# A hybrid SSD, attention and PEER layer: the query/key/value projection, its norm, rotation and transposes as one stage, with modulation units on four column groups

## The reference

```python
mod_ctx = jax.nn.silu(c_ctx) @ w_ada[l] + b_ada[l]          # 6 parts of 1024: shift1, scale1, gate1, shift2, scale2, gate2
mod_lat = (jax.nn.silu(c) @ w_ada[l] + b_ada[l])[:, None, :]
h = modulate(rmsnorm(x, lp['norm1_w']), shift1, scale1)
proj = h @ lp['w_in']                                        # z, xbc, dt_f, dt_b, q, k, v, g_a, g_b
q = rmsnorm(q.reshape(bsz, t, N_HEADS, HEAD_DIM), lp['q_norm_w'])
k = rmsnorm(k.reshape(bsz, t, N_KV_HEADS, HEAD_DIM), lp['k_norm_w'])
if ctx_k is None:                                            # context rows: no rotation, k and v are outputs
    keys, vals = k, v
else:
    q = axial_rope(q, pos[0], pos[1])
    keys = jnp.concatenate([axial_rope(k, pos[0], pos[1]), ctx_k], axis=1)
    vals = jnp.concatenate([v, ctx_v], axis=1)
y_b2 = attend(q, keys, vals) @ lp['w_attn_out']
```

## Time and profile before

| | us |
|---|---|
| median of 3 runs | 3220.26 (3216.32 to 3221.43) |
| the profiled execution | 3218.21 |
| its span, first to last instruction | 3216.4 |
| PE busy | 2690.7 (84%) |
| PEld busy | 2341.4 (73%) |
| DVE busy | 2256.1 (70%) |
| ACT busy | 1026.3 (32%) |
| POOL busy | 715.5 (22%) |
| stage 1 | 0 to about 57.4 |
| stage 2 | 57.4 to 184.6 |
| stage 3 | 184.6 to 302.9 |

### The profile page before, as it was taken

One profiled execution on the slowest core, in us unless ns is written; L12 is line 12 of the kernel. 1 busy time (PEld: TensorE's weight loads), 2 busy tenths in 40 slices (PEclk: granted clock), 3 DMA queues, 4 the chain that ended last, 5 costly groups with the idle time before them and its releaser, 6 DMA issues. The chain is left out here.

```text
span 3216.4 us, 41637 instructions
## 1 busy us (share of the span) xinstructions
PE 2690.7 (84%) x15241; PEld 2341.4 (73%) x15241; DVE 2256.1 (70%) x3693; ACT 1026.3 (32%) x1411; POOL 715.5 (22%) x597
## 2 busy tenths in 40 slices
PE   4968999998899999487767506679999999999995
PEld 3956777776777777377757506669998899988995
DVE  2252666665167777533329997769999999999997
ACT  3111444443233332322122105723333333333332
POOL 0000000000166666100000005623223333233330
PEclk7976999999999999788878758989999999999998
DMA  4253111111332332444210102399999999999995
GB/s 194 86 196 116 43 57 73 56 49 66 129 121 91 109 100 79 163 151 153 93 72 27 40 0 105 170 386 409 405 402 401 397 399 399 400 403 396 402 399 210
DMA packets 157182, 638.82 MB, mean 199 GB/s; under 512 B 13639, under 2 KB 77511, under 8 KB 93579
## 3 DMA queue, kind: packets, MB, share of 16 engines
q1 hardware_dynamic: 117676, 360.60, 30.2%
q0 software_dynamic: 39104, 276.71, 21.1%
q10 hardware_dynamic: 288, 0.03, 0.0%
HBM read 569.21 MB, written 68.21 MB: 198 GB/s over the span
## 5 line engine op out<-in xcount | busy, mean ns | idle before, releaser
L2022 POOL DMA_INDIRECT p_uv<-in_uv_rows,sidx x256 | 331.3, 1294 | 738.7 <-DVE p_ys L2174 661.7
L2036 PE MATMUL p_pa<-h2D,w_hi 128*128 128x384 f32 x1024 | 345.5, 337 | 15.5 <-PEq L2258 14.9
L2038 PE MATMUL p_pa<-h2D,w_lo 128*128 128x384 f32 x1024 | 344.9, 337 | 0.0
L2037 PE MATMUL p_pa<-h2D,w_hi 128*128 128x384 f32 x1024 | 344.7, 337 | 0.0
L104 DVE TENSOR_TENSOR w_lo<-w_raw,w_hi 128x2048 fp32r<-128x2048 f32 x64 | 152.3, 2383 | 267.2 <-ACT w_hi L99 267.0
L2174 DVE SCALAR_TENSOR_TENSOR p_ys<-p_uv,p_sw,p_ys 128x1024 f32<-128x1024 f32 x256 | 328.9, 1285 | 9.2
L2073 ACT ACTIVATE w_hi<-w_raw 128x2048 fp32r<-128x2048 f32 x126 | 241.5, 1917 | 273.8 <-PE p_py L2052 244.4
L2160 DVE CUSTOM_DVE_ANT_0 p_uv<-p_uv,hrow 128x1024 f32<-128x1024 f32 x256 | 307.3, 1219 | 14.4 <-DMA p_uv<-in_uv_rows,sidx 14.4
L2050 PE MATMUL p_py<-w_hi,p_wh 128*128 128x512 f32 x768 | 304.4, 396 | 7.3 <-DVE w_lo L2138 7.3
L2138 DVE TENSOR_TENSOR w_lo<-w_raw,w_hi 128x2048 fp32r<-128x2048 f32 x126 | 288.4, 2289 | 29.6 <-ACT w_hi L2073 29.6
L2051 PE MATMUL p_py<-w_lo,p_wh 128*128 128x512 f32 x768 | 305.1, 397 | 0.0
(11 more groups left out here) (341 smaller groups left out, 6075.5 us busy)
## 6 DMA issues: line engine op xcount, KB each, us to landing
w_raw<-in_w_stream SPq DMA_DIRECT2D x190, 1024.0 KB, 7.5
g_dram<-e_st SPq DMA_DIRECT2D x6, 4096.0 KB, 11.3
p_g<-g_dram SPq DMA_DIRECT2D x64, 384.0 KB, 16.2
q_ada<-in_w_ada SPq DMA_DIRECT2D x16, 1024.0 KB, 4.9
xc_dram<-c_xc SPq DMA_DIRECT2D x8, 1284.0 KB, 4.5
m_ada<-in_w_ada SPq DMA_DIRECT2D x6, 1024.0 KB, 19.5
s_xx<-xc_dram SPq DMA_DIRECT2D x8, 642.0 KB, 5.6
s_bc<-xc_dram SPq DMA_DIRECT2D x8, 642.0 KB, 7.0
```

The lines of the kernel that those rows point to most:

```text
L2022: nc.gpsimd.indirect_dma_start(uv[:, k % RING, :], None, K.uv_rows, bass.IndirectOffsetOnAxis(K.sidx[:, t, c:c + 1], 0)).then_inc(K.gather ...
L2036: nc.tensor.matmul(ps_a[m][:, :], wh[:, k, cols], K.h2D[0][:, k, :], start=k == 0, stop=False)
L2037: nc.tensor.matmul(ps_a[m][:, :], wh[:, k, cols], K.h2D[1][:, k, :], start=False, stop=False)
L2038: mm = nc.tensor.matmul(ps_a[m][:, :], wl[:, k, cols], K.h2D[0][:, k, :], start=False, stop=k == KD - 1)
```

## The change

Stages 2 and 3 become one, and nothing goes through `qkv_dram`.

- The dt weights are loaded and split in stage 1, into the free high and low buffers of slot 1. The high part of unit 1 is therefore made after the dt matmuls.
- As soon as a tile of a pair is in PSUM, ACT squares it there (`square`), DVE reduces, ACT takes the root (`root`), and DVE scales from PSUM and rotates (`normed`). POOL has multiplied the rotation tables with the norm weights before, so the rotated tiles need no product with the weight; the context tile has one. A piece is 8 query heads (pairs 0 and 1), or 4 key heads (pair 2, whose other half are the values, copied by ACT).
- PE transposes a piece in four blocks (`transposes`), at places in its queue that the table `follows` fixes: pieces 0 to 4 of a pair after the pair's tile 4 and after tiles 0, 2, 3 and 4 of the unit behind it. What has no such place is in `tail`. Two PSUM buffers take turns, and ACT evacuates them (`evacuate`).
- The 16 modulation units come in four batches of four (`rows`), all in row form on four column groups: after units 0, 1, 3 and 5, in the order shift2, scale2, gate1, gate2. Batches 0 and 1 are copied to SBUF and transposed (piece `COLS`), and DVE makes columns of them; batches 2 and 3 are the gates. SP loads each batch as a whole after the one before is used, in one queue with the stream's loads. The gates leave in eight stores.
- In stage 1 three of the eight buffers for modulation units are parts of `QT` and `KT`, which are allocated earlier.

```diff
-    ada = [K.raw[0], K.raw[1]] + [sb(f"m_ada{i}", [P, 8 * UC]) for i in range(6)]
+    qt, kt = K.QT[:, :, :].rearrange("p k t -> p (k t)"), K.KT[:, :, :].rearrange("p k t -> p (k t)")
+    ada = ([K.raw[0], K.raw[1], qt[:, 0:8 * UC], qt[:, 8 * UC:16 * UC], kt[:, 0:8 * UC]]
+           + [sb(f"m_ada{i}", [P, 8 * UC]) for i in range(3)])
+    dtw = sb("m_dtw", [P, KD * 64])
...
+            sp.dma_start(dtw[:, :], K.w_dt).then_inc(dtw_in, 16)
...
+                if t == 2:
+                    act.wait_ge(dtw_in, 16)
+                    nc.scalar.activation(K.whi[1][:, 0:KD * 64], dtw[:, :], ACT.Copy).then_inc(dtw_hi, 1)
...
+                if t == 3:
+                    dve.wait_ge(dtw_hi, 1)
+                    nc.vector.tensor_tensor(K.wlo[1][:, 0:KD * 64], dtw[:, :], K.whi[1][:, 0:KD * 64].bitcast(F32),
+                                            ALU.subtract).then_inc(dtw_lo, 1)
...
 def phase_tokens(nc, K, ctx):
...
-    ob = [sb(f"t_ob{t}", [P, 2 * UC]) for t in range(NT)]
+    PARTS = (3, 4, 2, 5)
-    ps_dt = ctx.enter_context(nc.psum_tensor("t_psdt", [P, NT, 64], F32))
-    ps_cum = [ctx.enter_context(nc.psum_tensor(f"t_cum{i}", [P, 3, NT * HEADS], F32)) for i in range(2)]
+    ps_row = ctx.enter_context(nc.psum_tensor("t_row", [P, 2 * UC], F32))
+    ps_dt = ps_row[:, 0:NT * 64].rearrange("p (t c) -> p t c", t=NT)
+    ps_t = [ctx.enter_context(nc.psum_tensor(f"t_pt{i}", [P, 4, P], F32)) for i in range(2)]
+    ps_cum = [ps_t[i][:, :, :].rearrange("p a c -> p (a c)")[:, 0:3 * NT * HEADS].rearrange("p (r x) -> p r x", r=3) for i in range(2)]
+    ada = [sb(f"t_ada{j}", [P, KD * UC]) for j in range(4)]
...
+    chunk = lambda i, t: 1 + NT * i + t
+    COLS = 1 + NT * PAIRS
+    AT = (4, 5, 7, 8, 9)
+    follows = {(1, 0): [0], (2, 1): [COLS]}
+    tail = []
+    for i in range(PAIRS):
+        for t in range(NT):
+            n = NT * (2 * i + 1) + AT[t]
+            if n < NT * N_TOK:
+                follows.setdefault((n // NT, n % NT), []).append(chunk(i, t))
+            else:
+                tail.append(chunk(i, t))
+    ORDER = [g for u in range(N_TOK) for t in range(NT) for g in follows.get((u, t), [])] + tail
+    turn = {g: n for n, g in enumerate(ORDER)}
...
+            def ada_load(b):
+                if b:
+                    sp.wait_ge(ada_used, b)
+                for j in range(4):
+                    sp.dma_start(ada[j][:, :], K.w_ada[4 * PARTS[b] + j]).then_inc(ada_in[j], 16)
...
+            ada_load(0)
...
+            S.load(sp, 3, 1)
+            ada_load(1)
+            S.load(sp, 4, 0)
+            S.load(sp, 5, 1)
+            ada_load(2)
+            S.load(sp, 6, 0)
+            S.load(sp, 7, 1)
+            ada_load(3)
+            S.load(sp, 8, 0)
+            sp.wait_ge(grow_done, 1)
+            for j in range(4):
+                for i in range(2):
+                    sp.dma_start(K.gates[0:2, i * D + j * UC:i * D + (j + 1) * UC], b_row[32 * j:32 * j + 2, i * UC:(i + 1) * UC]).then_inc(g_out, 16)
...
-            act.wait_ge(dtw_in, 16)
-            nc.scalar.activation(dtwh[:, :, :], dtw[:, :].rearrange("p (k c) -> p k c", k=KD), ACT.Copy).then_inc(dtw_hi, 1)
-            S.hi(act, 1, 1)
+            def square(i, t):
+                act.wait_ge(mm_done, NT * i + t + 1)
+                n = (QH if i < 2 else KH) * HD
+                nc.scalar.activation(sq[t % 2][:, 0:n], ps[t][:, 0:n], ACT.Square).then_inc(sq_done, 1)
+                if i == 2:
+                    nc.scalar.activation(K.vals[:, t, :], ps[t][:, n:2 * UC], ACT.Copy).then_inc(v_done, 1)
+            def root(i, t):
+                c = NT * i + t
+                act.wait_ge(ms_done, c + 1)
+                n = QH if i < 2 else KH
+                nc.scalar.activation(ss[c % 2][:, 0:n], ss[c % 2][:, 0:n], ACT.Sqrt).then_inc(rt_done, 1)
+            def evacuate(g):
+                n = turn[g]
+                act.wait_ge(tr_done, n + 1)
+                nc.scalar.activation(out, ps_t[n % 2][:, :, :], ACT.Copy).then_inc(tr_ev, 1)
...
+            act.wait_ge(dt_mm, 1)
+            S.hi(act, 1, 1)
             act.wait_ge(cum_mm, 2)
+            S.hi(act, 2, 0)
+            for i in range(PAIRS):
+                square(i, 0)
+                square(i, 1)
+                if i == 0:
+                    evacuate(0)
+                root(i, 0)
+                square(i, 2)
+                root(i, 1)
+                square(i, 3)
+                root(i, 2)
+                evacuate(chunk(i, 0))
+                square(i, 4)
+                S.hi(act, 2 * i + 3, 1)
+                if i == 0:
+                    act.wait_ge(ada_used, 2)
+                    nc.scalar.activation(row[:, :], ps_row[:, :], ACT.Copy).then_inc(row_ev, 1)
+                root(i, 3)
+                evacuate(chunk(i, 1))
+                root(i, 4)
+                if i == 0:
+                    act.wait_ge(modc_done, 2)
+                    act.sem_inc(tr_ev, 1)
+                for t in range(2, NT):
+                    evacuate(chunk(i, t))
+                if i < PAIRS - 1:
+                    S.hi(act, 2 * i + 4, 0)
...
+            def normed(i, t):
+                c, g = NT * i + t, chunk(i, t)
...
+                dve.wait_ge(sq_done, c + 1)
+                link(nc.vector.tensor_reduce(s, heads(sq[t % 2][:, 0:n * HD]), axis=AX.X, op=ALU.add))
+                nc.vector.tensor_scalar(s, s, 1.0 / HD, EPS, ALU.mult, ALU.add).then_inc(ms_done, 1)
+                dve.wait_ge(rt_done, c + 1)
+                link(nc.vector.reciprocal(s, s))
+                nc.vector.tensor_tensor(heads(x), heads(ps[t][:, 0:n * HD]), s.unsqueeze(2).to_broadcast([P, n, HD]),
+                                        ALU.mult).then_inc(x_read, 1)
+                dve.wait_ge(x_read, c + 1)
+                if turn[g] >= 3 and g >= 4:
+                    dve.wait_ge(tr_done, turn[g - 3] + 1)
...
+                axes = x.rearrange("p (h a f d) -> p h a f d", h=n, a=2, f=2)
+                a, b = axes[:, :, :, 0, :], axes[:, :, :, 1, :]
+                for f, (j, op) in enumerate(((0, ALU.subtract), (1, ALU.add))):
+                    link(nc.vector.tensor_tensor(t1[:, 0:n], a, tab(0, j), ALU.mult))
+                    link(nc.vector.tensor_tensor(t2[:, 0:n], b, tab(1, 1 - j), ALU.mult))
+                    last = nc.vector.tensor_tensor(qo[:, :, :, f, :], t1[:, 0:n], t2[:, 0:n], op)
+                    if f == 0 or i == 2:
+                        link(last)
+                    else:
+                        last.then_inc(src_done, 1)
+                if i == 2:
+                    nc.vector.tensor_copy(kd[:, :, 1, :], kd[:, :, 0, :]).then_inc(src_done, 1)
...
+            nc.vector.memset(ps_row[:, :], 0.0).then_inc(row_zero, 1)
...
+            S.lo(dve, 1, 1)
+            dve.wait_ge(cum_exp, 2)
...
+            for i in range(PAIRS):
+                for t in range(4):
+                    normed(i, t)
                 S.lo(dve, 2 * i + 3, 1)
+                normed(i, 4)
+                if i == 0:
+                    dve.wait_ge(small, 32)
+                    dve.wait_ge(tr_done, turn[COLS] + 1)
+                    for b in range(2):
...
+                if i < PAIRS - 1:
+                    S.lo(dve, 2 * i + 4, 0)
+            dve.wait_ge(brow_in, 8 * 16)
+            dve.wait_ge(ada_used, 4)
+            nc.vector.tensor_tensor(b_row[:, :], ps_row[:, :], b_row[:, :], ALU.add).then_inc(grow_done, 1)
...
+            def rows(b):
+                for j in range(4):
+                    pe.wait_ge(ada_in[j], 16 * (b + 1))
+                for kd in range(KD):
+                    for j in range(4):
+                        nc.tensor.matmul(ps_row[32 * j:32 * j + 2, b % 2 * UC:(b % 2 + 1) * UC], K.silu_c[:, kd, :],
+                                         ada[j][:, kd * UC:(kd + 1) * UC], start=(kd == 0), stop=(kd == KD - 1))
+                pe.drain().then_inc(ada_used, 1)
+            def transposes(g):
+                n = turn[g]
+                if g == 0:
+                    pe.wait_ge(ck_done, 2)
+                elif g == COLS:
+                    pe.wait_ge(row_ev, 1)
+                else:
+                    pe.wait_ge(src_done, g)
+                if n >= 2:
+                    pe.wait_ge(tr_ev, n - 1)
+                for j in range(4):
+                    if g == 0:
+                        src = ckd[:, j, :, :].rearrange("p c d -> p (c d)")
+                    else:
+                        src = (row if g == COLS else qr[g % 3])[:, j * P:(j + 1) * P]
+                    mm = nc.tensor.transpose(ps_t[n % 2][:, j, :], src, K.ident[:, :])
+                mm.then_inc(tr_done, 1)
+            def unit(u):
+                i, s = u // 2, u % 2
+                S.ready(pe, u)
                 wh, wl = (x[s][:, :].rearrange("p (k c) -> p k c", k=KD) for x in (K.whi, K.wlo))
                 for t in range(NT):
-                    if s == 0 and not isinstance(i, int):
```

(34 more changed lines are left out.)

349 lines of the change are left out of this document (109 added, 240 removed).

## The result

| us | before | after |
|---|---|---|
| median (range, executions) | 3219.5 (3216.3 to 3221.4, 4) | 3126.2 (3125.2 to 3130.3, 4) |
| profiled execution (span) | 3218.2 (3216.4) | 3125.2 (3123.5) |
| projection's start to attention's first instruction | 245.5 | 151.5 |
| everything behind that | 2913.5 | 2914.3 |

The ratio is 0.971, 95% interval 0.970 to 0.973: faster. The forecast was 3128.0 with 3116 to 3145 around it. The time that was saved lies wholly in the stretch that the prediction marked off: 245.5 - 151.5 = 94.0 us. Of these 0.4 us came back ahead of it, where the stage before ended later, and 0.8 us behind it.

A forecast was written before the change was run, and what follows sets the result against it. PE was taken to bound the projection. One TensorE queue to 192.05 us, then a DVE tail, starts attention at 210.7 instead of 302.9: 3220.3 - 92.2 = 3128 us, range 3116 to 3145.

The forecast's parts named there:

- the 0.7 wait: Pair 0, before the fourth tile's transposes: PE waits about 0.7 us for the modulation columns, the stage's tightest place.
- The bound: Merged stage up to unit 5: one TensorE queue sets the time, ending at 192.05 us with unit 5's transposes.
- The rival that DVE is the bound: Merged stage: at 6.0 us a DVE tile, 10 to 14 us longer, 3140; chance 0.13.
- Transposes: PE's queue before the last batch: 13 groups of four transposes at 0.7 us each, 9.1 in all.
- the lower bound of 6.5: PE's queue: low end for all 13 transpose groups, at 0.5 us each; the upper end was 13.
- all waits hidden: PE's queue: the low case for one group of four transposes, 0.5 us.
- the 13.7 in the text: PE's queue: time charged for unit 1 from its start at 104.25, in placing PE's wait at 136.7.
- the rival: Modulation loads arrive late, at 4.9 us per 1 MB: 6 us more, 3134; chance 0.06.
- The slow rival: Row batches and transposes hold PE's clock down from 86 us to unit 5's end: 106 us more, 3234; chance 0.03.
- closed no circle: Rival on ACT's queue: waits for PE and DVE prevent overlap, 30 to 35 us come back, 3160; chance 0.06.
- Tail: Stage's end: DVE late, needing 3.9 us a tile against 2.86; gate rows added at 205.1, attention at 210.7.
- The handover: Stage's end: 3.5 us from the last gate store to attention, after 2.1 for seven more store issues.

The follow-up runs named there:

- Experiments 7: Kernel after with the rotation of the query heads left out, so less DVE work: 3125.5 us.
- experiment 4: Kernel after with the two loops of a row batch exchanged, so each column group finishes its unit before the next begins: 3154.4 us.
- Experiments 1 to 3: Kernel before with row-form batches in the old third stage, 3198.0 us; then ACT's row copy moved, 3197.0; then three batches' loads left out too, 3179.6.
- Experiment 5: Kernel after with the third to fifth transposes of pairs 0 and 1 earlier in PE's queue: 3141.5 us.
- experiment 3: Kernel before with row-form batches in the old third stage, ACT's copy moved, and only the first batch's weights loaded: 3179.6 us.
- experiment 2: Kernel before with row-form batches in the old third stage, all loads kept, ACT's row copy moved behind a root: 3197.0 us.
- experiments 5 and 7 to 10: Kernel after with: transposes earlier, 3141.5 us; query rotation out, 3125.5; key rotation out too, 3125.4; unit 7's split later, 3125.8; also first gates and root earlier, 3123.2.

## Why the prediction was right

The forecast's terms and the trace (us):

| step | forecast | trace after |
|---|---|---|
| PE's first matmul | 57.45 | 57.83 |
| dt matmuls | 25.6 | 25.6 |
| unit 0, sums, batch 0 | 15.7 + 1.6 + 3.9 | 15.6 + 1.8 + 3.9 |
| unit 1 starts | 104.25 | 104.72 |
| four transposes inside a unit / at its end | 0.7 / 0.7 | 0.35 / 0.5 to 0.7 |
| PE waits for the modulation columns | 0.7 | 0.50 |
| DVE tile, eight heads / four | 4.9 / 3.9 | 4.77 / 3.73 |
| lo of unit 6 starts | 180.4 | 178.15 |
| unit 5 begins | 177.9 | 175.43 |
| unit 5 and its transposes end | 192.05 (192.8 with the 0.7 wait, which the sum left out) | 190.11 |
| gate rows added | 205.1 | 202.73 |
| first store to attention | 5.6 | 6.5 |
| attention starts | 210.7 | 209.25 |

- **The bound.** Until unit 5 the stage is PE's queue, as forecast. Experiments 7 (DVE work out: nothing) and 4 (PE work in: all of it, and more) show it from both sides. The rival that DVE is the bound falls; it also rested on PSUM as a source, and that costs nothing here.
- **Transposes.** They were sized too high. Between two tiles the matmul at 107.51 and the next of the unit at 107.98 are 0.47 apart, 0.12 of it the pitch, so four transposes cost 0.35 us and not 0.7. The prediction charged 0.16 for the matmul ahead to finish; the rows show the transpose starting one pitch behind it (107.63), with no such end to wait for. Seven of the eight groups in such places cost 0.35 each, and the one that waits for ACT 0.55 beside its wait. The five at a unit's end, with its drain, cost 0.5 to 0.7 beyond the 0.25 that the end costs anyway. That is some 6.1 us for the 13, where 9.1 were charged, and less than the lower bound of 6.5: what was taken as "all waits hidden", 0.5 a group, was still too high. This is why unit 5 begins 2.5 us earlier than forecast, although unit 1 began 0.5 later and took 0.5 longer than the 13.7 in the text.
- **Loads.** A load of 1 MB of a batch landed 10.5 us after its issue in the median and 14.6 at most, and no matmul waited for `t_ada`. Asked for at 104.54, 132.19 and 165.91, as forecast (104.3, 132, 166.6), they are wanted at 119.8, 155.6 and 190.1. Experiments 1 to 3 show what the rival would have looked like: where nothing of the projection lies between asking for a batch and using it, the loads cost 16 us, the low clock behind PE's waits included.
- **Clock.** It was 1.0 from 98 us to the tail. The slow rival did not come: row batches and transposes between the units do not hold the clock down. Experiment 5 shows another way to 1.2 GHz, by waits of 6 and 4 us; in the kernel after PE is never short of work for more than 0.50 us until the tail.
- **Overlap.** ACT's waits in its queue for PE and for DVE closed no circle; the largest that reached PE was the 0.50 us.
- **Tail.** DVE's part came out right to 0.1 us (22.4 forecast from the end of lo of unit 6 to the end of the gates' addition, 22.3 measured), but that is luck. The prediction gives tile 0 of the third pair 2.8 us and then counts 3.8 for it (182.7 to 186.5); it took 3.3. The three tiles behind it took 12.5 and not 11.7, because one root stands in ACT's queue behind the hi part of unit 7 and DVE waits 1.43 us for it (193.29), a wait that the prediction did not have. The handover was 0.9 us too low. The eight issues take 2.33 us, 2.07 more than one, as forecast (2.1); from the last one to attention it is 4.4 where 3.5 was read from one store.

So attention starts 1.45 us earlier than forecast, out of 2.3 less and 0.9 more; counted from the stage's start, which came 0.4 later than in the kernel before, 1.8 us earlier. The median stands 1.9 us below the forecast. The bound, the queue and the waits were as predicted; that the number is so near is in part luck, since the transposes (3 us less) and the handover (0.9 more) erred in opposite directions.

What stays open: which part of the 16.2 us of experiment 3 is the serial loading and which is the clock. With the loads (experiment 2) PE idles 10.1 to 12.2 us ahead of each batch behind the first, 33.1 in all, and these three batches take 6.0, 5.4 and 4.9 us, 5.4 more together than at the full clock (3.64 each). With one load that chain is no longer the bound, so the 5.4 can't be subtracted from the 16.2: DVE is busy nearly throughout, PE waits 3.3, 6.7 and 10.6 us for it, and the granted clock is 1.0 only from 216 to 231 us and 0.50 from 245 on. A run with the weights in further buffers, loaded ahead, would separate the two; it was not made.

## What to carry to other kernels

When a stage is bound by PE and the next by a mixture of half-clock weight loads and vector work, sum PE's queue of the merged stage matmul by matmul and lay the vector engine's tiles beside it. Put operations that must wait behind work that PE can do anyway: transposes two or three tiles too early cost 13 us here, the two waits of 6 and 4 us and the low clock behind each. A large wait on the page is worth nothing until the longest chain is known: to cut DVE's longest wait from 15.4 us to 6.2 bought 0.6.

## What was not expected of the hardware

- Matmul records of one column group (128 x 2 against 256 columns) start 0.216 us apart at the full clock, in a unit alone as in one group after another (experiment 4). Where the next records belong to another group they run beside: at a border four pairs do, and with four groups in turns all do, so that a unit takes 0.91 us in place of 3.62.
- PE's granted clock was 1.00, then 0.66, then 0.50 within one wait of 5.8 us, and stayed low for some 5 us of work behind it (experiment 5), which made it cost 8 us.
- A batch and the units around it change between column groups and the full array. The gap behind each batch is 0.26 us, which is also what a unit takes to its successor (0.23 to 0.26). Ahead of a batch four transposes take 0.56 to 0.58 us (119.23 to 119.81), ahead of a unit's matmul 0.38 to 0.39 (136.91 to 137.29 and 175.04 to 175.43). The Trainium skill (TensorEngine Tiling (Array Packing), Key Properties) says that a change of the tiling mode drains TensorE; by these rows its price here is at most 0.2 us on the way into a batch, and nothing beyond the usual gap on the way out.
- The projection stage started at 57.4 to 60.8 us behind a stage with the same work, and the clock rose to full at different times in the first unit: six executions with the same queue up to there (the kernel after, experiments 5 and 7 to 10) asked for batch 1 between 46.7 and 47.7 us behind the stage's start. Steps of under 1 us could be read only from one event to another within the tail, not from the start of the span.
